# A decoder layer's output projection by seven block products instead of eight, weight differences on GpSimd, and bias rows read already reversed

## The reference, cut to what matters

```
h    = rms_norm(x, attn_norm_g);  proj = h @ w_in
oa   = hgrn2_mixer(...)                       # gated recurrence, 4 heads of 128
ob   = dsa_mixer(...)                         # indexer, top-128 keys, attention with rel_bias by distance
mix  = sigmoid(gate_a) * (oa @ w_up_hgrn) + sigmoid(gate_b) * (ob @ w_up_attn)
x    = x + mix @ w_o                          # (512 x 1024) @ (1024 x 1024): the output projection
x    = x + square(relu(rms_norm(x, mlp_norm_g) @ w_mlp_in)) @ w_mlp_out
out  = rms_norm(x, final_norm_g)
```

## Time and profile before

| | |
|---|---|
| median of three runs | 743.21 us (743.0 to 743.22) |
| the profiled execution: its time, its span | 743.21 us, 741.4 us |
| span that lies on PE in the chain that ended last | 92% |
| busy share PE, DVE, ACT, POOL | 98%, 72%, 48%, 14% |
| PE's waits for another engine | 10.3 us, of which 7.8 before its first instruction |
| TensorE clock granted, mean | 0.997 |

### The profile page before, as it was taken

One profiled execution on the slowest core, in us unless ns is written; L12 is line 12 of the kernel. 1 busy time (PEld: TensorE's weight loads), 2 busy tenths in 40 slices (PEclk: granted clock), 3 DMA queues, 4 the chain that ended last, 5 costly groups with the idle time before them and its releaser, 6 DMA issues.

```text
span 741.4 us, 9808 instructions
## 1 busy us (share of the span) xinstructions
PE 724.2 (98%) x3498; PEld 605.1 (82%) x3498; DVE 531.5 (72%) x805; ACT 358.8 (48%) x576; POOL 101.0 (14%) x128
## 2 busy tenths in 40 slices
PE   5999999999999999999999999999999999999996
PEld 4788878888788888888888888888888888888885
DVE  4676998888799873336634696867768595968964
ACT  6463544765643555543313754545363554545442
POOL 6021240014431354200200100000000000000002
PEclk9999999999999999999999999999999999999998
DMA  7422122120422111112622333241505041332002
GB/s 295 145 84 86 57 90 82 58 85 30 143 85 83 61 57 57 57 58 85 255 86 76 152 114 114 86 142 57 170 8 194 24 156 70 113 114 85 30 1 113
DMA packets 20723, 71.50 MB, mean 96 GB/s; under 512 B 2344, under 2 KB 3536, under 8 KB 20688
## 3 DMA queue, kind: packets, MB, share of 16 engines
q1 hardware_dynamic: 19120, 67.88, 26.2%
q10 hardware_dynamic: 1568, 3.15, 1.2%
HBM read 68.91 MB, written 2.11 MB: 96 GB/s over the span
## 4 chain that ended last, share of the span: by engine, by line
PE 92%; DVE 3%; ACT 2%; DMA 1%; issue 1%; SPq 0%; POOL 0%; POOLq 0%; DVEq 0%; ACTq 0%
PE bank L1492 28%; PE bank L1494 27%; PE bank L1493 27%; PE bank L1500 2%; PE bank L1722 2%; PE bank L1623 2%; DMA xs<-x 1%; PE bank L1704 1%; PE bank L1703 1%; PE bank L1674 0%; PE bank L1635 0%; PE bank L1688 0%; DVE wlo L1000 0%; PE bank L1613 0%; PE bank L1614 0%
## 5 line engine op out<-in xcount | busy, mean ns | idle before, releaser
L1492 PE MATMUL bank<-hTh,whi 128*128 128x512 f32 (+1 forms) x456 | 182.4, 400 | 1.7 <-DVE hTl L1020 1.3
L1494 PE MATMUL bank<-hTh,wlo 128*128 128x512 f32 (+1 forms) x456 | 177.8, 390 | 0.0
L1493 PE MATMUL bank<-hTl,whi 128*128 128x512 f32 (+1 forms) x456 | 177.7, 390 | 0.0
L1492 PEld LDWEIGHTS bank<-hTh,whi 128*128 128x128 f32 (+1 forms) x456 | 85.4, 187 | 21.5 <-issue 4.2
L1494 PEld LDWEIGHTS bank<-hTh,wlo 128*128 128x128 f32 (+1 forms) x456 | 85.2, 187 | 18.5
L1493 PEld LDWEIGHTS bank<-hTl,whi 128*128 128x128 f32 (+1 forms) x456 | 85.4, 187 | 17.9 <-issue 1.0
L1000 DVE TENSOR_TENSOR wlo<-raw,whi 128x1024 fp32r<-128x1024 f32 x51 | 66.0, 1296 | 31.6 <-ACT whi L674 31.5
L674 ACT CAST whi<-raw 128x1024 fp32r<-128x1024 f32 x58 | 60.4, 1043 | 40.9 <-PE bank L1494 40.6
L1492 PE MATMUL bank<-whi,ah 128*128 128x512 f32 x196 | 76.2, 389 | 0.0
L1493 PE MATMUL bank<-wlo,ah 128*128 128x512 f32 x196 | 76.2, 389 | 0.0
L1494 PE MATMUL bank<-whi,al 128*128 128x512 f32 x196 | 76.2, 389 | 0.0
(11 more groups left out here) (233 smaller groups left out, 1380.0 us busy)
## 6 DMA issues: line engine op xcount, KB each, us to landing
raw<-slabs SPq DMA_DIRECT2D x87, 512.0 KB, 3.3
br<-slabs SPq DMA_DIRECT2D x32, 512.0 KB, 3.3
xs<-x SPq DMA_DIRECT2D x4, 512.0 KB, 5.5
y<-x ACTq DMA_DIRECT2D x1, 2048.0 KB, 8.6
out<-ys SPq DMA_DIRECT2D x3, 512.0 KB, 2.6
bt<-bias_rows ACTq DMA_DIRECT2D x1, 1024.0 KB, 6.9
cst<-consts SPq DMA_DIRECT2D x1, 608.0 KB, 9.1
fg<-final_g SPq DMA_DIRECT2D x1, 512.0 KB, 7.1
```

Source lines behind the costliest of these rows:

```text
L1492: pe.matmul(dst, lh, rh, start=start, stop=False)
L1493: pe.matmul(dst, lh, rl, start=False, stop=False)
L1494: return pe.matmul(dst, ll, rh, start=False, stop=stop)
```

## The change

**Output projection.** mix is taken as 2 x 2 blocks (256 tokens by 512 features) and w_o as 2 x 2 blocks (512 by 512; `wq` 11, 12, 21, 22, two slabs each). Seven products replace the eight; each is 24 matmuls (2 token tiles, 4 k, 3). Products 0, 1 and 6 take blocks of mix as they are, products 2 to 5 take sums of blocks. The sums:

- of mix (one tile of 128 x 1024 each): `s1`, `s2` on DVE, `s3` and the second `s1` on POOL; each is then rounded by ACT (`s_hi`) and subtracted by DVE (`s_lo`)
- of weights: four differences of two slabs each on POOL (`t_sum`), eight instructions of 128 x 1024, written to two spare tiles or over loaded blocks
- of results: products 0, 2 and 3 feed more than one block of y; ACT copies halves out (`u1`, `p5`), DVE adds (`y_add`, `u2`), and POOL adds to y (`y_sum`, ten instructions of 128 x 512)

The eight `wo` slabs no longer go through `raw`: SP loads them at once, when the last `gb` slab has been used, to the place of `hTh` and `hTl`. There are 14 weight tiles to round and subtract instead of 8. The transposes of y for the MLP are spread: four columns of blocks between the parts of the last product, the rest after it and inside the first hidden slab. POOL's memsets come after them.

**Bias.** ACT writes each row 128 times to memory (1.5 MB), so that the reading can step back by one for each partition. The `flip` matmuls and their copies are gone; POOL waits for the read.

**Start.** The last token tile: ACT squares one half, DVE the other (after it has scaled tile 2), POOL adds them; DVE scales one half, ACT the other, and only then ACT rounds slab 0. DVE's two small operations on `vec` come after the eight `hTl`.

**Waits.** Where a product's input is split just before (`hf` 0, `iq`, `ua`, `ub`), PE waits for the rounded part only, does h·h and l·h, and then waits for the rest.

The diff, cut to its core:

```diff
@@ SP
+            b, u = tiles[n_gb + 7][0]
+            sp.wait_ge(full[b], u + 1)
+            for k, col in (("11", 0), ("12", 4), ("21", 2), ("22", 6)):
+                for c in range(2):
+                    sp.dma_start(wq[k][c][:, :], slabs[n_wo + col + c]).then_inc(wq_in[k], 16)
...
@@ POOL
+            def t_sum(k, c):
+                if k == "1":
...
+                    to, a_, b_ = wt[c], wq["12"][c], wq["11"][c]
...
+                pool.tensor_tensor(to[:, :], a_[:, :], b_[:, :], ALU.subtract).then_inc(S["tw_done"], 1)
...
+            t_sum("1", 0)
+            t_sum("1", 1)
+            pool.wait_ge(S["mix_done"], 4)
+            pool.tensor_tensor(four(s3), mix_part(tha3, 0, 0), mix_part(tha3, 1, 0), ALU.subtract).then_inc(S["sw3_done"], 1)
+            t_sum("2", 0)
+            t_sum("2", 1)
+            t_sum("3", 0)
+            t_sum("3", 1)
+            pool.wait_ge(S["sw2_done"], 1)
+            pool.wait_ge(S["sl_done"], 1)
+            pool.tensor_tensor(four(s1), mix_part(tha3, 0, 1), four(s2), ALU.subtract).then_inc(S["sw4_done"], 1)
+            def y_sum(r_, c, q, of):
+                yy = wo_y(r_, c, q)
+                pool.tensor_tensor(yy, yy, of[q][:, :], ALU.add).then_inc(S["yu_done"], 1)
...
@@ ACT, start
+                w = D if t < NT - 1 else D // 2
+                square(xs3[:, t, 0:w], w, ssx[:, t:t + 1], D ** -0.5)
+            act.wait_ge(S["rs_done"], NT)
+            act.wait_ge(S["sqd_done"], 1)
+            act.activation(xs3[:, NT - 1, D // 2:D], xs3[:, NT - 1, D // 2:D], ACT.Copy,
+                           scale=rsx[:, NT - 1:NT]).then_inc(S["xna_done"], 1)
             hi(0)
@@ DVE, output projection (v counts the weight tiles)
+                if v == 0:
+                    dve.wait_ge(S["mix_done"], KD_)
+                    dve.tensor_tensor(four(s1), mix_part(tha3, 1, 0), mix_part(tha3, 1, 1), ALU.add).then_inc(S["sw1_done"], 1)
...
+                lo(n_wo + v + AHEAD)
...
+                if v == 7:
+                    s_lo(2, s3)
...
+                if v == 9:
+                    s_lo(3, s1)
@@ PE
-                if k == "flip":
...
-                    pe.matmul(bank[b][:, :], flip, bt[:, 512 * h:512 * h + 512], start=True, stop=True).then_inc(full[b], 1)
+            for p in range(6):
+                if p < 2:
+                    pe.wait_ge(S["mxl_done"], 4 * p + 4)
+                else:
+                    pe.wait_ge(S["sl_done"], p - 1)
+                for c in range(2):
+                    pe.wait_ge(*split_done(n_wo + 2 * p + c))
+                    for q in range(2):
+                        ins = wo_product(p, q, c)
```

More of the change, by code:

```diff
@@ L230, in build @@
         r = 0
+        n_wo = AT_SLAB["wo", 0]
         proj_use = [0] * 4
-        for n in range(NPLAN):
+        for n in range(n_wo):
             if isinstance(tiles[n], list):
@@ new lines, in y_sum @@
+            def y_sum(r_, c, q, of):
+                yy = wo_y(r_, c, q)
+                pool.tensor_tensor(yy, yy, of[q][:, :], ALU.add).then_inc(S["yu_done"], 1)
+            pool.wait_ge(y_in, 16)
+            for q in range(2):
+                b, u = wo_bu[0][q]
+                pool.wait_ge(free[b], u + 1)
+                y_sum(0, 0, q, u1)
+            t_sum("4", 0)
+            t_sum("4", 1)
+            for q in range(2):
+                pool.wait_ge(S["p5_done"], q + 1)
+                y_sum(0, 1, q, p5)
@@ new lines, in _ @@
+            for q in range(2):
+                pool.wait_ge(S["yu_done"], 3 + q)
+                b, u = wo_bu[3][q]
+                pool.wait_ge(free[b], u + 1)
+                y_sum(0, 1, q, u2)
+            for q in range(2):
+                pool.wait_ge(S["y7_done"], q + 1)
+                y_sum(1, 1, q, u2)
+            for q in range(2):
+                b, u = wo_bu[4][q]
+                pool.wait_ge(free[b], u + 1)
+                y_sum(1, 0, q, u2)
+            b, u = mlp_bank[MLP_K[-1]]
@@ L1320, in _, with s_lo, y_add @@
                             do_side(s)
-            for q, k in enumerate(MLP_K):
+            def s_lo(k, of):
+                dve.wait_ge(S["sh_done"], k + 1)
+                dve.tensor_tensor(sl[k][:, :], of[:, :], sh[k][:, :].bitcast(F32), ALU.subtract).then_inc(S["sl_done"], 1)
+            def y_add(p, q, r_, c):
+                b, u = wo_bu[p][q]
+                wait_full((b, u))
+                yy = wo_y(r_, c, q)
+                return dve.scalar_tensor_tensor(out=yy, in0=bank[b][:, :], scalar=0.5, in1=yy, op0=ALU.mult, op1=ALU.add)
@@ L1325, in final @@
+            for q in range(2):
+                dve.wait_ge(S["yu_done"], 9 + q)
+                y_add(6, q, 1, 0).then_inc(free[wo_bu[6][q][0]], 1)
+                if q == 0:
+                    h_lo_(0)
+                    h_lo_(1)
+            for q in range(2, KD_):
+                h_lo_(q)
+            lo(NV + 2)
             def final(t):
@@ L1729, in do_side, with turn_y, wo_product @@
                         transposes(BK[s][q], [ob3[:, t, q * P:(q + 1) * P] for t in range(NT)])
-            for n in range(NPLAN):
+            def turn_y(k, ts):
+                b, u = mlp_bank[k]
+                for t in ts:
+                    ins = pe.transpose(bank[b][:, t * P:(t + 1) * P], y3[:, t, k * P:(k + 1) * P], ident)
+                return ins
+            def wo_product(p, q, c):
+                s = (n_wo + 2 * p + c) % SLOTS
+                wh, wl = slab_view(whi, s, 2), slab_view(wlo, s, 2)
+                b, u = wo_bu[p][q]
+                ah_, al_ = wo_a[p]
+                for kk in range(2):
+                    if c == 0 and kk == 0:
+                        wait_free((b, u))
+                    k = 2 * c + kk
+                    ins = three(bank[b][:, :], ah_[:, k, q * P:(q + 1) * P], al_[:, k, q * P:(q + 1) * P], wh[:, kk, :],
+                                wl[:, kk, :], k == 0, k == 3)
+                if c:
+                    ins.then_inc(full[b], 1)
+                return ins
+            for n in range(n_wo):
                 for p in range(PARTS):
```

342 lines of the change are left out of this document (251 added, 91 removed).

## The result

The changed kernel takes 760.49 us (759.5 to 760.5, four runs) against 743.11 us (742.63 to 743.22, four runs): the ratio is 1.0233, 95% interval 1.0221 to 1.0245. The profiled execution has a span of 758.8 us, 17.3 more than before. The forecast was 763.0 us.

What follows compares the result with a forecast made beforehand. PE was taken to bound the kernel (92% of the last chain). Span 741.4 + 16.1 (projection) + 2.0 (clock) + 2.2 (start) - 0.5 (flips) = 761.2, plus 1.8 beyond the span: 763.0 us, range 750 to 769.

Steps and rivals of the forecast that it cites:

- The first rival: Output projection: DVE and POOL don't hold each other, so POOL's work hides; 741.2 us, chance 0.08.
- whoever comes first is done first: DVE two-SBUF-input and POOL SBUF-reading instructions: the earlier one finishes, the other waits; 2.24 of POOL's 2.38 us exclusive.
- The second rival: Output projection: exclusion bites but DVE mostly comes first, no slow clock; 756.5, 752 or 750.7 us, chance 0.08.
- The exclusion: Output projection: DVE's and POOL's SBUF work must alternate, so PE waits; +16.1 us with savings, 19.8 by itself.
- W0: Start of the output projection on PE, 357.51 us in the kernel before; the forecast counts times from it.
- The second wait: Output projection, before product 4: PE waits another 8 us or so for DVE's s_lo.
- rounded part first: Matmuls at hf 0, iq, ua, ub: starting on the rounded part was costed at 0.
- SP's later loads: MLP raw slabs 0 to 3, fg and the final load are asked for later: 0; without cover 3.3 us.
- DVE's order: Output projection: s_lo(2) and s_lo(3) queue behind a subtraction waiting for ACT, 1.0 us lost each; +2.0 us.
- Clock: Output projection: PE's matmuls run slowly after long idle stretches, at half clock; +2.0 us (0 to 5.4).
- Start: Kernel start: halved last tile and later rounding of slab 0 delay PE's second slab; +2.2 us (0.9 to 2.6).
- Flips: Before attention: removed flip matmuls save PE 3.5 us, but DVE sets the time; -0.5 us (-1.4 to +0.5).

Runs made afterwards that it cites:

- write_only: Changed kernel with each of POOL's sums in the output projection replaced by memsets that read nothing from SBUF: 740.38 us, ratio 0.9965 to the kernel before.
- Twice: Changed kernel with POOL computing the first two weight differences twice: 764.43 us, ratio 1.0282 to the kernel before.
- defer: Changed kernel with POOL waiting for all of mxl before its third weight difference: 760.09 us, ratio 1.0233 to the kernel before.
- start_undone: Changed kernel with the start of the kernel before put back: 757.65 us, ratio 1.02 to the kernel before.
- bias_alone: Kernel before with the bias edit only: 741.7 us, ratio 0.9982.
- slo_first: Changed kernel with s_lo(2) and s_lo(3) moved ahead of the DVE subtraction that waits for ACT's rounding: 757.45 us, ratio 1.0196 to the kernel before.
- start_alone: Kernel before with the start edit only: 745.37 us, ratio 1.0033.
- start_hi_early: Kernel before with the start edit only, but ACT rounds slab 0 before waiting for the last root: 743.69 us, ratio 1.001.
- seven_dve: Changed kernel with DVE forming all weight differences and both POOL sums of mix, the old start and DVE's queue reordered: 751.32 us, ratio 1.0118 to the kernel before.

## Why the prediction was right

*What decides.* The step "a DVE instruction with two SBUF inputs and a POOL instruction that reads SBUF don't run side by side" held, and write_only shows it to be the cause: its removal takes 20 us off. The first rival (POOL's work hides) fell with it; write_only, at 740.4, is where it had put the kernel (741.2). Twice and defer show that the exclusive times add up. The other half of the step, "whoever comes first is done first", is not a full account: mostly the engines took turns, but now and then DVE's queue passed a waiting POOL instruction (last section). The second rival had DVE mostly first and no slow clock; both stalls and the slow clock came, so it fell too.

*The exclusion.* Sized at W0 + 17 for the last mxl and W0 + 42.5 for product 4, it measured W0 + 15.2 and W0 + 40.0. POOL began at 345.78, W0 - 13.6, and 28.7 us later the last mxl was there, for 31.1 forecast. Since POOL began late, two of the 14 sums and differences were already done: by the same prices 12 of them and the rest make 25.5 us, so 3.2 us of gaps and not 4.5. From there to product 4 it was 24.8 us for 25.4. The second wait was mis-stated: by the forecast's own terms it would have been 42.5 - 17 - 16.3 = 9.2, not 8. It measured 5.7, for product 1 ran at half the clock for 2.6 us longer and product 4 was ready sooner; that doesn't enter the total. From product 4 to the end of the first hidden slab I had 26.7 and 2.0 for the clock; it measured 28.7. The whole term with the clock was +18.1 and is 757.65 - 741.70 = 15.95 (start_undone against bias_alone, so the rounded part first and SP's later loads are in it). This is the term that was too large, by 2.15 us.

*DVE's order.* 2.0 us; slo_first gained 3.0 in the kernel with exclusion (2.7 within the projection), write_only's two waits are 1.7.

*Clock.* +2.0 taken, 2.0 seen behind the wait before product 4. The slow stretch behind the first wait was swallowed by the second, as argued (not tried by itself). I had missed that the start can dip too.

*Start.* +2.2 against 2.4 by start_alone: about 1.6 of late data, and the rest from the clock in most executions. That the total was met is partly luck: I had all of it as late data, with DVE's `hTl` from 16.1 (they began at 15.67 in start_alone) and the two small operations, and nothing for the clock. start_hi_early shows ACT's rounding as the larger part of what was lost.

*Flips.* -0.5 taken, -1.25 measured, near the bound of 1.4 that DVE's gaps gave. The 0.5 us that I had put against it for POOL's seven subtractions didn't show.

*Sum.* -1.25 + 2.4 + 15.95 = 17.1, and the change cost 17.4: the parts add up within what can be measured. Rounded part first, the 1.5 MB of bias rows and SP's later loads were costed at nothing; bias_alone bounds the second, the others were not tried alone. Term by term the forecast was too high by 2.15 (exclusion and clock) and 0.75 (flips) and too low by 0.2 (start): 2.7 in all, for the 2.5 between 763.0 and 760.5.

## What to carry to other kernels

Before work is moved to an engine that looks idle, look for the slowest instances of the engines' short instructions, not for their means: two maxima of 2.4 and 2.8 us in a page of 0.7 and 1.2 told here that POOL's slack wasn't free. Then count the exclusive time of both engines as one queue and compare it with the matmuls that cover it: seven products saved 5.4 us of PE and put some 34 us of POOL's exclusive time (10 x 2.24 and 10 x 1.16) in front of the engine that feeds it. And a saving on PE ahead of a stage that another engine sets is worth only that engine's gaps.

## What the runs showed that was not expected

*A DVE queue without gaps can keep POOL out for many instructions.* I had taken it as first come, first done. In the changed kernel POOL's sum at 380.35 took 5.52 us for 2.4, while three DVE instructions passed, of which two had come after it. In seven_dve it stood from 366.90 until DVE's first gap, some 16 us, while DVE's 1024-column instructions kept their 1.22:

```profile
366.24 1.22 DVE L1435 TENSOR_TENSOR sl<-s,sh 128x1024 fp32r<-128x1024 f32 x1
367.37 1.22 DVE L1467 TENSOR_TENSOR wq<-wq,wta 128x1024 f32<-128x1024 f32 x1
...
382.13 1.22 DVE L1122 TENSOR_TENSOR wlo<-wq,whi 128x1024 fp32r<-128x1024 f32 x1
384.53 0.69 DVE L1442 SCALAR_TENSOR_TENSOR y<-bank,y 128x512 f32<-128x512 f32 x1 [1.18 <-POOL y L718]
```

But a queue without gaps doesn't always do this. In defer POOL's difference came 0.17 us after a DVE instruction of 1024 columns had begun, was let in at its end, and then the engines took turns, one instruction each, with no gap in DVE's queue either. DVE first, then POOL:

```profile
364.64 1.22 DVE L1506 TENSOR_TENSOR s<-tha 128x1024 f32<-128x1024 f32 x1
365.78 3.42 DVE L1170 TENSOR_TENSOR wlo<-wq,whi 128x1024 fp32r<-128x1024 f32 x1
369.11 3.41 DVE L1509 TENSOR_TENSOR s<-s,tha 128x1024 f32<-128x1024 f32 x1
```

```profile
364.81 3.30 POOL L740 TENSOR_TENSOR wq<-wq,wta 128x1024 f32<-128x1024 f32 x1 [11.08 <-DVE mxl L1258]
368.06 3.38 POOL L740 TENSOR_TENSOR wq<-wq,wtb 128x1024 f32<-128x1024 f32 x1
```

The changed kernel's pairs at 352.88 and 360.87 took such turns as well. So what two queues do to each other isn't settled by their lengths: once each waits for the other they alternate, and a POOL instruction that comes to a DVE queue that hasn't been held can be passed many times. What decides between the two is open. It was let in when it came 0.17 and 0.22 us (defer, 364.81 and 379.25) after the start of the DVE instruction under way, and passed at 0.23 (380.35) and 0.66 (366.90); no run varied that moment by itself.

The Trainium skill (SBUF — State Buffer, "Who interferes with whom") calls the shared pair an exclusive lock and says that issue order decides who blocks. The rows agree for single instructions and for the turns; for POOL's sums at 380.35 and 366.90, passed by DVE instructions that came later, the measurement differs, and decides.

*Behind a wait of 1.9 us at the start the clock is sometimes low.* Behind a wait of 1.87 us before the first matmul the granted clock was 0.53 from 18 to 21.6 us, in the changed kernel's profile; behind 1.91 us in start_alone's it was 1.00; behind 1.86 us in slo_first's it was 1.00 too. Behind 0.81 us (the kernel before) and 1.03 us (start_hi_early) it was 1.00 in the profiles, and the mean clock of every execution was 0.997 or above. The same start gave both, and start_alone's times spread by 1.1 us; what decides is open.
